# Four transformer blocks and a fifth on one core: matmul operands moved to other byte offsets in SBUF

## The reference, cut to what matters

```python
h = layer_norm(ALPHA * h + mixer(h), ln_g[i], ln_b[i])        # four times: ssd, fox, mla, s5
x = x + mixed_attention(rms_norm_2(x, g_mix)) @ w_out         # then once
x = x + memory_cross_attention(rms_norm_2(x, g_cross), rms_norm_2(mem, g_mem), ...)
x = x + (silu(conv(g)) * u) @ w_down                          # g, u = split(rms_norm_2(x, g_ffn) @ w_up)
return rms_norm_2(x, g_final)
```

## Time and profile before

| | before |
|---|---|
| timed runs | 3517.45, 3521.31, 3524.25 us (median 3521.31) |
| profiled execution, first to last instruction | 3518.1 us |
| mean granted TensorE clock | 0.988 |
| TensorE matmuls busy | 3383.7 us, 96% of the span, 18,278 instructions |
| TensorE weight loads busy | 2912.4 us, 83% |
| VectorE busy | 2387.5 us, 68% |
| ScalarE busy | 1550.1 us, 44% |
| GpSimd busy | 240.6 us, 7% |
| HBM read | 638.02 MB, 183 GB/s over the span |

### The profile page before, as it was taken

The page is one execution under the profiler, slowest core; times in us unless marked ns, Lnnn a source line. Parts: engine busy times, 40 slices in busy tenths (PEclk is TensorE's granted clock), DMA queues, the critical chain, the costliest instruction groups (busy, mean ns, idle before and its releaser), DMA issues.

```text
span 3518.1 us, 48946 instructions
## 1 busy us (share of the span) xinstructions
PE 3383.7 (96%) x18278; PEld 2912.4 (83%) x18278; DVE 2387.5 (68%) x3140; ACT 1550.1 (44%) x1909; POOL 240.6 (7%) x273
## 2 busy tenths in 40 slices
PE   8899999999999998999999999999998999999998
PEld 6788888878888877887999988888996888888886
DVE  5777777775555665666899877666566766556555
ACT  3444444444444344443687743443434434434342
POOL 0000000010000023721100000000001100000000
PEclk9999999999999999999999999999999999999999
DMA  6455555545444443443433456656664555555553
GB/s 225 180 203 204 208 207 203 205 178 189 178 175 173 172 170 144 163 172 108 152 128 110 152 179 214 221 214 235 249 246 167 180 191 191 181 189 180 192 189 119
DMA packets 90903, 645.03 MB, mean 183 GB/s; under 512 B 10768, under 2 KB 10848, under 8 KB 13856
## 3 DMA queue, kind: packets, MB, share of 16 engines
q1 hardware_dynamic: 83376, 605.07, 47.4%
q0 software_dynamic: 7408, 38.33, 3.2%
HBM read 638.02 MB, written 5.32 MB: 183 GB/s over the span
## 4 chain that ended last, share of the span: by engine, by line
PE 61%; issue 16%; DVE 13%; DVEq 4%; ACT 2%; DMA 2%; POOL 1%; ACTq 0%; POOLq 0%; SPq 0%
PE banks L726 17%; PE banks L728 17%; PE banks L727 17%; DVE WL L693 4%; DMA raw<-in_stream 2%; DVE xc L1421 1%; ACT WH L685 1%; POOL WL L709 1%; PE banks L1064 1%; PE banks L744 1%; PE banks L1590 1%; PE banks L745 1%; PE banks L746 1%; DVEq L2663 1%; PE banks L3318 1%
## 5 line engine op out<-in xcount | busy, mean ns | idle before, releaser
L693 DVE TENSOR_TENSOR WL<-raw,WH 128x2048 fp32r<-128x2048 f32 (+2 forms) x565 | 1193.1, 2114 | 669.4 <-ACT WH L685 656.3
L685 ACT ACTIVATE WH<-raw 128x2048 fp32r<-128x2048 f32 (+2 forms) x575 | 1019.4, 1775 | 1111.5 <-DMA raw<-in_stream 686.0
L726 PE MATMUL banks<-WH,XH 128*128 128x512 f32 (+2 forms) x2784 | 1058.7, 380 | 39.1 <-POOL WL L709 10.3
L728 PE MATMUL banks<-WH,XL 128*128 128x512 f32 (+2 forms) x2784 | 1035.2, 372 | 0.0
L727 PE MATMUL banks<-WL,XH 128*128 128x512 f32 (+2 forms) x2784 | 1034.2, 371 | 0.0
L726 PEld LDWEIGHTS banks<-WH,XH 128*128 128x128 f32 x2784 | 527.5, 189 | 127.8 <-issue 34.5
L728 PEld LDWEIGHTS banks<-WH,XL 128*128 128x128 f32 x2784 | 526.9, 189 | 81.0
L727 PEld LDWEIGHTS banks<-WL,XH 128*128 128x128 f32 x2784 | 527.9, 190 | 78.2 <-issue 1.7
L726 PE MATMUL banks<-WH,YH 128*128 128x512 f32 x976 | 391.5, 401 | 2.8 <-DVE YL L2765 2.8
L727 PE MATMUL banks<-WL,YH 128*128 128x512 f32 x976 | 386.3, 396 | 0.0
L728 PE MATMUL banks<-WH,YL 128*128 128x512 f32 x976 | 386.0, 396 | 0.0
(11 more groups left out here) (442 smaller groups left out, 3582.1 us busy)
## 6 DMA issues: line engine op xcount, KB each, us to landing
raw<-in_stream SPq DMA_DIRECT2D x571, 1024.0 KB, 4.8
gain<-in_gains POOLq DMA_DIRECT2D x9, 1024.0 KB, 5.5
arow<-acs_scratch POOLq DMA_DIRECT2D x8, 1024.0 KB, 4.8
offs<-in_ln_b POOLq DMA_DIRECT2D x4, 1024.0 KB, 8.4
acc<-in_x SPq DMA_DIRECT2D x2, 1024.0 KB, 7.3
raw<-in_stream SPq DMA_DIRECT2D x4, 512.0 KB, 5.9
turns_scratch<-trig POOLq DMA_DIRECT2D x16, 128.0 KB, 2.7
turns<-turns_scratch POOLq DMA_DIRECT2D x16, 128.0 KB, 2.4
```

Of the source, the lines that this page charges most:

```text
L685: nc.scalar.activation(WH[:, n.first % PARTS, at], raw[:, n.first % RAWS, at], ACT.Copy).then_inc(hi_ready, 1)
L693: nc.vector.tensor_tensor(WL[:, n.first % PARTS, at], raw[:, n.first % RAWS, at], WH[:, n.first % PARTS, at].bitcast(F32), ALU.subtract).t ...
L726: nc.tensor.matmul(out, xh[:, k0 + k, at], wh[:, k, lo:hi], start=start, stop=False)
L728: ins = nc.tensor.matmul(out, xl[:, k0 + k, at], wh[:, k, lo:hi], start=False, stop=stop)
```

## The change

It changes where buffers lie, and nothing of what is computed or of the order of the work. `XH` gets 16 bytes behind each row block, `WH` 16 bytes behind each place and `WL` 32 bytes behind each place. An unused buffer `apart` of 32 bytes stands in front of `YH`. To make room, `rhot` and `rtab` no longer have buffers of their own: they lie in `small`, which is used for other things before and after.

```diff
-    XH = sb("XH", [P, KC, T], F32R)
+    XH = sb("XH", [P, KC, T + 4], F32R)[:, :, 0:T]
     XL = sb("XL", [P, KC, T], F32R)
     raw = sb("raw", [P, RAWS, SLOT])
-    WH = sb("WH", [P, PARTS, SLOT], F32R)
-    WL = sb("WL", [P, PARTS, SLOT], F32R)
+    WH = sb("WH", [P, PARTS, SLOT + 4], F32R)[:, :, 0:SLOT]
+    WL = sb("WL", [P, PARTS, SLOT + 8], F32R)[:, :, 0:SLOT]
...
+    sb("apart", [P, 8])
     YH = sb("YH", [P, 4, T], F32R)
     YL = sb("YL", [P, 4, T], F32R)
...
-                rhot = sb("rhot", [48, N], within=s3)
                 rvec = sb("rvec", [MIX_HEADS, N], within=s3)
-                rtab = sb("rtab", [48, 16], within=s3)
             memk = sb("memk", [P, MEM_HEADS, T], within=s2)
             memv = small[:, :, :].rearrange("p (t c) n -> p t (c n)", t=TT)
+            rhot = small[0:48, 0:8, :].rearrange("p c n -> p (c n)")
+            rtab = small[0:48, 8, 0:16]
...
-        nc.tensor.matmul(bank[7][0:16, :], rtab[:, :], rhot[:, :], start=True, stop=True).then_inc(bias_done, 1)
+        nc.tensor.matmul(bank[7][0:16, :], rtab, rhot, start=True, stop=True).then_inc(bias_done, 1)
...
-        pool.dma_start(rtab[:, :], a["table"]).then_inc(mix_loaded, 16)
-        pool.dma_start(rhot[:, :], a["hot"]).then_inc(mix_loaded, 16)
+        pool.dma_start(rtab, a["table"]).then_inc(mix_loaded, 16)
+        pool.dma_start(rhot, a["hot"]).then_inc(mix_loaded, 16)
```

## The result

The changed kernel takes 3537.24 us (median of 13 runs, 3529.48 to 3544.42), beside 3522.87 us for 13 runs of the kernel before. The ratio is 1.0043, with a 95% interval of 1.0033 to 1.0052: slower by some 15 us. The prediction was 3493 us and faster.

A forecast was written before the change was run, and what follows sets the result against it. TensorE's matmul pace was taken as the bound; 21.8 us on Y plus 8.5 us on X made 30.3 us, of which 0.93, 28 us, came off 3521 to give 3493 us, with a range of 3445 to 3540 us.

The forecast's parts named there:

- What bounds the kernel: Whole kernel: TensorE, matmuls busy 3383.7 of 3518.1 us, so a change of its pace goes into the span almost whole.
- The 0.93: Whole kernel: share of the 30.3 us of saved TensorE time taken to arrive in the span, giving 28 us.
- X products: 10,656 matmuls on `XH`, `XL` with mixed offsets after the change: 0.8 ns saved each, 8.5 us gained.
- S5 and the narrow products: Products narrower than 512 columns, priced within the X products at the same 0.8 ns saved a matmul.
- Y products: 3,456 matmuls on `YH`, `YL`, put at multiples of 128 bytes: 6.3 ns saved each, 21.8 us gained.
- if the weights' new offsets undo it: Lower bound on the Y products: no gain at all from moving `YH` and `YL`.
- the slower rival: `XH` products pay what `YH` paid, 55 us lost, Y gain whole or halved: about 3560 us; chance 0.20.
- The large gain: All matmuls: spread offsets give back much of the fixed 13.1 ns a step, about 3445 us; chance 0.18.
- Nothing moves: Whole kernel: offsets can't matter, or gain and loss cancel; time stays at 3521 us; chance 0.12.
- Splits, map, `LH`: ScalarE/VectorE splits stay hidden even 10% dearer; bias map in `small` costs nothing; `LH`, `LL` matmuls under 1 us, costed at nothing.
- The signs that I named: 512-column steps: `YH` 227 ns or less right, 232 and more wrong; `XH` 225 to 228 forecast, 230 to 233 slower case.
- The period of eight over row blocks: Sign on `XH`: steps differing by row block with period eight would show that the distance between the streams decides.

The follow-up runs named there:

- e1: Kernel before with `YH`, `YL` moved by 96 unused bytes to a multiple of 256 bytes from the weights, bias map in `small`: 3501.99 us, ratio 0.9944.
- e6: Kernel before with `XH`, `XL` shifted 64 and `YH`, `YL` 80 bytes inside buffers made 128 bytes longer, bias map in `small`: 3535.68 us, ratio 1.0045.
- e4: Kernel before with activation and weight buffers all 32 bytes above a multiple of 128, all distances 0, bias map in `small`: 3505.31 us, ratio 0.9948.
- e9: Kernel before with `XH`, `XL` 128 and `YH`, `YL` 256 bytes from the weights' place, bias map in `small`: 3529.26 us, ratio 1.0024.
- e13: Kernel before with `YH`, `YL` moved by 224 bytes, to distance 128 modulo 256 from the weights, bias map in `small`: 3519.27 us, ratio 0.9995.
- e11: Kernel before with only the bias map's inputs `rhot` and `rtab` moved into `small`: 3518.26 us, ratio 0.9992.
- e5: Kernel before with `XH`, `XL` shifted 16 and `YH`, `YL` 48 bytes inside buffers made 128 bytes longer, bias map in `small`: 3537.58 us, ratio 1.0060.
- e7: Kernel before with `XH`, `XL` shifted 96 and `YH`, `YL` 112 bytes inside buffers made 128 bytes longer, bias map in `small`: 3537.8 us, ratio 1.0052.
- e10: e1 with activations used 64 bytes further on in S5; the longer `XH` buffer put `XL` at distance 128 in every stage: 3520.61 us, ratio 0.9996 to before.
- e14: e10 with `XL` back at distance 0, and high and low parts both at 64 in S5 only: 3498.86 us, ratio 0.9941 to the kernel before.
- e15: Kernel before with `XH`, `XL` both at distance 96 and `YH`, `YL` both at 224, bias map in `small`: 3553.97 us, ratio 1.0092.
- e2: Kernel before with only the row blocks of `XH` 16 bytes further apart, bias map in `small`: 3543.01 us, ratio 1.0054.
- e8: Kernel before with `WL` alone moved 64 bytes, all other operands at distance 0, bias map in `small`: 3532.99 us, ratio 1.0037.

## Why the prediction was wrong

**What bounds the kernel: right.** TensorE's pace goes into the span nearly whole: 14.9 us more in the steps of the table, 14.1 us more of span; in e1 21.3 us less busy, 20.4 us less span. The 0.93 that I took was, if anything, a little low.

**X products, the step that failed.** "For a mix of all distances I take that nearest price that speaks of a distance without a loss, 0.8 ns saved." That price was of `LH` at 256 columns, and I carried it to 512. Nor was it "the same offset" as that of `YH`: both lie 32 bytes above a multiple of 128, but by the sizes of the buffers `LH` is 32 from the weights modulo 256 and `YH` 160. The measured price is +4.2 ns on 6,048 matmuls, 25.7 us lost. The two widths can answer to one placement with opposite signs: with high parts at 64 and low at 192, -6.7 ns at 256 columns and +5.1 ns at 512 (e6). The earlier trace rows was the row of the same width and spoke of a loss; it should have set the term for the 512-column products and the earlier trace rows that for the 256-column ones. With 4.2 ns on 6,048 and -1.6 ns on the 2,304 of S5 the X term becomes a loss of 22 us in place of a gain of 8.5. Less the 5.8 us of Y that is 16, and 0.93 of it the 15 us that the time shows.

**S5 and the narrow products: right where the row was of their width.** 0.8 ns saved was taken, 1.6 ns measured in S5 (3.9 us); at 384 columns the step rose by 1 ns (178.8 to 179.8), which the prediction's price had with the wrong sign.

**Y products, 21.8 us: the right size of the wrong thing.** The difference between the earlier trace rows was real and is won back in full when `YH` and `YL` are at distance 0 (e1: 19.4 us of steps, ratio 0.9944). I wrote that the reader sees one operand at a multiple of 128 and one 32 above it, and took the multiple of 128 for the cause. e4 shows that alignment is not it, e9 and e13 that 128 is too short a period and 256 is not. In the changed kernel `YH` stands 128 bytes from place 0 of `WH` and drifts by 16 with each place, so it never meets `WH` at 0; `WL` it meets at 0 in place 2 alone. Only 5.8 us came. The bound "if the weights' new offsets undo it" was named, but the forecast took Y whole, and only the slower rival halved it. It should have weighed in the forecast: the table of offsets in front of the prediction shows that neither `YH` nor `YL` keeps one distance from the weights after the change.

**The slower rival: right in kind.** It priced X at the cost of the earlier trace rows, 55 us lost less 15 won, some 40 us. Measured are 25.7 lost on 512 columns and 14 us in all. It was too dear since it applied 6.3 ns to 10,656 matmuls of all widths, where 6,048 pay and those paid 4.2. Its mechanism, plain alignment, is not the one at work. I gave it 0.20, although it had the only row of the right width for it.

**The large gain: fallen.** None of the kernels brought the mean 512-column step on X or Y clearly under 226.7 ns (226.6 is the lowest stretch, in e1). The part of a step that doesn't depend on the width, 13.1 ns, is what distance 0 leaves, not the worst meeting. That it came out the same at 256 and at 512 columns proved nothing, since these two rows had given the price of a column; the one test was 384, 12.8. The Trainium skill ("TensorE: Matmul & The Clock Gate", section "Back-to-back issue gap") gives N / 2.4 + 2.5 ns for an isolated matmul, as an estimate 215.8 for 512 columns; no run here, with a load for each matmul, came near it. At 256 columns e6 comes down to 113.3 where that rule gives 109.2.

**Nothing moves: fallen.** Addresses alone took the time from 0.9941 to 1.0092. The Trainium skill ("SBUF — State Buffer", section "Who interferes with whom") gives TensorE's moving operand and its weight load independent ports. The runs disagree, as far as pace is concerned: the step is 226.7 ns or up to 234.3 by the placement of the two alone, with no other engine's work changed.

**Splits, map, `LH`: right.** 1,917 and 2,291 ns; e11 at 0.9992; on `LH` and `LL` 119.3 ns and 119.2 at 256 columns, 120.2 and 120.9 at 192.

The signs that I named told it correctly: steps on `YH` still at 232, steps on `XH` at 230 to 233, "the slower case". The period of eight over row blocks did not come out cleanly. Modulo 256 it takes sixteen row blocks of 16 bytes to come round, the distance to four places of weights moves too, and a badly placed matmul also slows its neighbours.

## What to carry to other kernels

When TensorE is the bound and each matmul loads another stationary piece, compare the start-to-start step between buffers of one shape in the trace, and take the addresses of both operands modulo 256; here the 512-column float32r products want them equal, for high and low parts alike, and one unused buffer of 96 bytes was worth 20 us in 3,520. Do not spread operands over offsets in hope of an average, and do not carry the price of a placement from one width to another. After any edit of a buffer's size, work out every operand's address behind it again: twice here (e5 to e7, and e10) 128 bytes added behind a buffer changed what the run measured.

## What the runs showed of the hardware that was not expected

- A 512-column step takes 226.6 to 227.2 ns at distance 0 modulo 256, also with every operand 32 bytes above a multiple of 128 (e4). At every other placement tried (distances of 16 to 240, among them 128) the mean of the three matmuls is 229.9 to 234.3 ns. A single one can be cheap: 227.0 ns in e5, with `YL` loaded at 48.
- At 256 columns distance 0 is not the best: 120.0 ns, 113.3 with high at 64 and low at 192 in SSD; S5 went from 122.0 to 120.2 with both at 64 (e14). But not every distance helps there: with both at 96 (e15) the S5 steps average 122.8.
- Matmuls whose own operands lie well pay when a neighbour's do not (e2, e8, e10). In e10 the matmul ahead of the badly placed one pays, while that one's piece is loaded.
- An explanation is that the moving stream and the load of the next weights read the same memory in parallel and get in each other's way by a pattern that repeats after 256 bytes. That is argued from these steps and not shown; no run looked into the memory itself. Not tried: all pairs of distances for high and low parts at 512 columns, so that some pair under 226.7 ns can't be excluded, and a placement that gives the 256-column products of SSD their distance while the rest keeps 0.
